# Carrying the state of a gated linear attention once per 128 tokens instead of once per 64

## The chip, the cores and the metric

The kernel runs on one core of a Trainium2 chip. TensorE multiplies matrices, VectorE (DVE), ScalarE (ACT) and GpSimd (POOL) do elementwise work, SyncE (SP) issues the loads. The metric is the device time of one execution in microseconds, median of several runs; less is better.

## The reference

A residual decoder layer for 512 tokens of width 1024: two token mixers side by side (GLA with 4 heads, keys of 128 and values of 256; HGRN2 with 8 heads, keys and values of 128), gates, an output projection, a convolutional feed-forward part, and norms. The change touches only the core of both mixers:

```python
def chunk_gated_linear_attn(q, k, v, log_g, scale):   # chunks of CHUNK = 64 tokens
    b = jnp.cumsum(log_g, axis=3)                     # within a chunk
    b_ref = b[..., CHUNK // 2 - 1:CHUNK // 2, :]
    b_last = b[..., -1:, :]
    scores = einsum(q * exp(b - b_ref), k * exp(b_ref - b))   # then causal mask
    o_intra = einsum(scores, v)
    chunk_state = einsum(k * exp(b_last - b), v)
    chunk_decay = exp(b_last)
    S_next = chunk_decay * S + chunk_state            # scan over the chunks
    o_inter = einsum(q * exp(b), S_prev)
    return o_intra + o_inter
```

After it come an RMS norm per head, a silu gate, the merge of both mixers and `merged @ w_out`.

## The kernel before

Everything large is a product in three terms: an fp32 matrix is split into a high part and a rest, `three` issues hi x hi, lo x hi and hi x lo. `unit` does one slice of 128 output columns over all 512 tokens: 24 matmuls of 512 columns. ScalarE makes `w_hi` from a loaded slice (`split_hi`), VectorE `w_lo` (`split_lo`); SyncE's next load into the ring of three raw buffers waits for `w_lo`. Before some loads SyncE also waits for a row of `ada_acc`, which VectorE adds up between its other work.

The mixers run as four groups (group 0 written out, groups 1 to 3 in a loop of the same code). A group has 18 units, n = 0 to 17, and three heads: h = 0 is a GLA head, h = 1 and 2 are HGRN heads. The order on every engine is written out by hand: each engine's `group` has a list of what it does ahead of or behind unit n. Between the units TensorE does small blocks: `turn` and `score` of head 0 behind unit 7, `chunk_states(0)` behind 8, `outputs` of head 0 behind 10, `turn` of heads 1 and 2 behind 11, `chunk_states` of head 1 behind 12 and of head 2 behind 13, `score` of both behind 14, `outputs` of both behind 15, and the sums of `ada_acc` behind 16. Behind unit 1 stand `low_rank` and the transposes of the group before (`merged_turn`). Units 2 to 5, 8 to 11 and 14 to 17 are quads that wait for all four `w_lo` of the quad.

A tile is 128 tokens, two chunks. The tensors of one head lie with the key channel on the partitions and the 512 tokens in the free dimension: `ks`, `qs` (scaled about the middle of the chunk, for the scores), `kp` (scaled to the end of the chunk, for the state), `qe` (scaled from its start, for the output from the state). ScalarE makes their exponentials (`exps`), VectorE multiplies `kp` and `ks` with the key (`times_k`), GpSimd `qs` and `qe` with the query (`times_q`). `turn` transposes `kp`, ScalarE takes it to `kT`. `score` makes four matmuls per tile, each with 32 array columns; VectorE copies the scores under the mask to `sT`. `chunk_states` multiplies `kT` with `v`, 64 rows (one chunk) at a time, seven times per head; VectorE runs the recurrence over seven states (`states`). `outputs` adds `sT` times `v` and, chunk by chunk, `qe` times the state, the latter with 64 array columns each. Matmuls on these operands are in plain fp32, and each shows as two records in the profile. `gla_rms` (ScalarE) squares and sums the GLA outputs, `gla_y` (VectorE) applies the norm and the gate; `outputs(1, 2)` overwrites the same PSUM banks and waits for `gla_y`.

## Time and profile before

| | |
|---|---|
| median of 3 runs | 943.22 us (942.72 to 943.66) |
| the profiled execution | 943.3 us, its span 941.6 us |
| granted TensorE clock, mean | 0.987 |
| TensorE busy | 911.9 us (97%) |
| VectorE, ScalarE, GpSimd busy | 501.3, 456.2, 155.6 us |
| chain that ended last | TensorE 87%, every other engine at most 3% |

Busy time of TensorE says that it had a matmul under way, not that it ran at its peak. The groups take the span from about 55 to 517 us; the output projection and the feed-forward part follow. The stretches of groups 1, 2 and 3 start at 171.23, 290.11 and 408.99 us, with the transposes of the group before behind unit 1. The third group below is group 2, from 290.11 to 408.99 us.

### The profile page before, as it was taken

What the parts mean: (1) busy time and instruction counts of PE and PEld (TensorE: products, weight loads), DVE (VectorE), ACT (ScalarE), POOL (GpSimd) and SP (SyncE); (2) the same over time, 40 slices, a digit from 0 to 9 for tenths busy, and PEclk for the clock granted to TensorE, in tenths of its full rate; (3) what the DMA queues carried; (4) which work ended last, traced back from release to release, by engine and by line L of the source; (5) the groups of instructions that cost most, each with busy time, mean ns of one, the idle gap of its engine ahead of it and who ended that gap; (6) DMA issues with size and microseconds to landing.
All of it is one profiled execution on the core that took longest, in us unless ns stands there. A gap on an engine that the chain in (4) does not pass through costs nothing.

```text
span 941.6 us, 13572 instructions
## 1 busy us (share of the span) xinstructions
PE 911.9 (97%) x4852; PEld 738.8 (78%) x4852; DVE 501.3 (53%) x690; ACT 456.2 (48%) x699; POOL 155.6 (17%) x146
## 2 busy tenths in 40 slices
PE   5998999999999999999999998999999999999997
PEld 4776788887888878888787776888888888888885
DVE  3545683457634476354764366744544544633327
ACT  5475554555645656456564263634333333523224
POOL 2010232002330123301232100121111121100000
PEclk8998999999999999999999999999999999999999
DMA  9946251662416624166230660433333333242202
GB/s 320 374 134 190 66 147 46 180 179 68 113 45 178 178 67 106 50 178 176 69 111 23 140 196 23 121 104 110 90 90 109 91 90 110 79 140 96 90 0 90
DMA packets 146830, 112.16 MB, mean 119 GB/s; under 512 B 4494, under 2 KB 138138, under 8 KB 146538
## 3 DMA queue, kind: packets, MB, share of 16 engines
q1 hardware_dynamic: 146288, 111.37, 39.9%
q8 instruction: 21, 0.34, 0.1%
q0 software_dynamic: 160, 0.20, 0.1%
q10 hardware_dynamic: 345, 0.13, 0.1%
q14 instruction: 16, 0.12, 0.1%
HBM read 107.49 MB, written 4.20 MB: 119 GB/s over the span
## 4 chain that ended last, share of the span: by engine, by line
PE 87%; DVE 3%; issue 3%; ACT 3%; DMA 2%; ACTq 0%; POOL 0%; SPq 0%; POOLq 0%; DVEq 0%
PE ps L1318 27%; PE ps L1320 26%; PE ps L1319 26%; PE ps L1438 2%; PE ps L1468 2%; DMA hres<-xT_saved_dram 1%; PE ps L1463 1%; PE ps L1352 1%; DMA raw<-in_w_in_dram 1%; DVE w_lo L893 1%; PE ps L1548 1%; PE ps L1420 1%; PE ps L1460 0%; ACT w_hi L557 0%; PE ps L1406 0%
## 5 line engine op out<-in xcount | busy, mean ns | idle before, releaser
L893 DVE TENSOR_TENSOR w_lo<-raw,w_hi 128x1024 fp32r<-128x1024 f32 x142 | 186.5, 1325 | 124.4 <-ACT w_hi L557 123.7
L1318 PE MATMUL ps<-h_hi,w_hi 128*128 128x512 f32 x608 | 238.9, 393 | 5.2 <-DVE h_lo L1235 3.3
L1320 PE MATMUL ps<-h_hi,w_lo 128*128 128x512 f32 x608 | 237.2, 390 | 0.0
L1319 PE MATMUL ps<-h_lo,w_hi 128*128 128x512 f32 x608 | 237.1, 390 | 0.0
L1318 PE MATMUL ps<-w_hi,h_hi 128*128 128x512 f32 x552 | 220.4, 399 | 5.4 <-DVE h_lo L933 3.8
L1319 PE MATMUL ps<-w_lo,h_hi 128*128 128x512 f32 x552 | 216.1, 392 | 0.0
L1320 PE MATMUL ps<-w_hi,h_lo 128*128 128x512 f32 x552 | 216.1, 391 | 0.0
L557 ACT ACTIVATE w_hi<-raw 128x1024 fp32r<-128x1024 f32 x142 | 146.9, 1052 | 70.7 <-PE ps L1320 48.8
L1318 PEld LDWEIGHTS ps<-h_hi,w_hi 128*128 128x128 f32 x608 | 114.5, 188 | 30.3 <-issue 4.5
L1319 PEld LDWEIGHTS ps<-h_lo,w_hi 128*128 128x128 f32 x608 | 114.6, 188 | 23.7 <-issue 0.2
L1320 PEld LDWEIGHTS ps<-h_hi,w_lo 128*128 128x128 f32 x608 | 114.4, 188 | 23.8
L1318 PEld LDWEIGHTS ps<-w_hi,h_hi 128*128 128x128 f32 x552 | 104.2, 189 | 32.9 <-issue 9.1
L1320 PEld LDWEIGHTS ps<-w_hi,h_lo 128*128 128x128 f32 x552 | 104.2, 189 | 22.5
L1319 PEld LDWEIGHTS ps<-w_lo,h_hi 128*128 128x128 f32 x552 | 104.4, 189 | 20.6
L824 ACT ACTIVATE conv<-ps,vecs 128x512 f32<-128x512 f32 x42 | 32.6, 778 | 130.4 <-PE ps L1320 130.4
L1247 DVE SCALAR_TENSOR_TENSOR conv<-ps,vecs,conv 128x511 f32<-128x511 f32 x44 | 32.9, 749 | 104.4 <-ACT conv L824 99.8
L544 POOL TENSOR_TENSOR prod<-conv 128x512 f32 x21 | 43.3, 2062 | 243.6 <-DVE conv L1251 243.6
L508 POOL TENSOR_TENSOR sg<-sg 128x256 f32<-128x256 f32 x32 | 26.1, 814 | 222.0 <-ACT sg L775 222.0
L775 ACT ACTIVATE sg<-ps 128x512 f32<-128x512 f32 x32 | 19.0, 595 | 76.4 <-PE ps L1320 76.3
L1061 DVE TENSOR_TENSOR gate<-ps,hnw_b 128x256 f32<-128x256 f32 x16 | 6.7, 421 | 55.2 <-ACT sg L775 55.2
L1251 DVE SCALAR_TENSOR_TENSOR conv<-ps,vecs,conv 128x510 f32<-128x510 f32 x44 | 32.9, 748 | 5.5 <-DVE conv L1247 0.2
L1092 DVE SCALAR_TENSOR_TENSOR ada_acc<-ada_w,cols,ada_acc 128x1024 f32<-128x1024 f32 x28 | 35.7, 1275 | 0.0
(205 smaller groups left out, 820.1 us busy)
## 6 DMA issues: line engine op xcount, KB each, us to landing
raw<-in_w_in_dram SPq DMA_DIRECT2D x68, 512.0 KB, 4.5
raw<-in_w_up_dram SPq DMA_DIRECT2D x44, 512.0 KB, 3.8
ada_w<-in_w_ada_dram SPq DMA_DIRECT2D x32, 512.0 KB, 4.4
raw<-in_w_down_dram SPq DMA_DIRECT2D x22, 512.0 KB, 3.3
ada_w<-in_w_ada_dram SPq DMA_DIRECT2D x8, 1024.0 KB, 9.1
raw<-in_w_out_dram SPq DMA_DIRECT2D x8, 512.0 KB, 4.7
x_tok<-in_x_dram SPq DMA_DIRECT2D x4, 512.0 KB, 5.2
w_first<-in_w_in_dram SPq DMA_DIRECT2D x8, 256.0 KB, 7.7
```

The lines of the kernel that those rows point to most:

```text
L508: pool.tensor_tensor(sg[:, j % 2, 0:2 * P], sg[:, j % 2, 0:2 * P], sg[:, j % 2, 2 * P:T], ALU.mult).then_inc(sides_made, 1)
L544: pool.tensor_tensor(prod[:, bass.ds(r * 3 + q, 1), :].rearrange("p a t -> p (a t)"), conv[:, 2 * q], conv[:, 2 * q + 1], ALU.mult).then_i ...
L557: act.activation(w_hi[:, slot(u)].rearrange("p k c -> p (k c)"), raw[:, raw_slot(u)].rearrange("p k c -> p (k c)"), ACT.Copy).then_inc(hi_ ...
L775: act.activation(sg[:, j % 2], bank, ACT.Sigmoid).then_inc(taken_act, 1)
L824: act.activation(conv[:, m], ps[:, m], ACT.Identity, bias=vecs[:, bass.ds(ch + V_CONVB, 1)], scale=vecs[:, bass.ds(ch + V_TAP2, 1)]).then_ ...
L893: dve.tensor_tensor(w_lo[:, slot(u)].rearrange("p k c -> p (k c)"), raw[:, raw_slot(u)].rearrange("p k c -> p (k c)"), w_hi[:, slot(u)].re ...
L1092: ins = dve.scalar_tensor_tensor(out=ada_acc[:], in0=ada_w[:, m % 2], scalar=c_act[:, m:m + 1], in1=ada_acc[:], op0=ALU.mult, op1=ALU.add)
L1247: dve.scalar_tensor_tensor(out=conv[:, m, 1:T], in0=ps[:, m, 0:T - 1], scalar=vecs[:, bass.ds(ch + V_TAP1, 1)], in1=conv[:, m, 1:T], op0=A ...
L1251: dve.scalar_tensor_tensor(out=conv[:, m, 2:T], in0=ps[:, m, 0:T - 2], scalar=vecs[:, bass.ds(ch + V_TAP0, 1)], in1=conv[:, m, 2:T], op0=A ...
L1318: pe.matmul(dst, a_hi, b_hi, start=start and i == 0, stop=False)
L1319: pe.matmul(dst, a_hi, b_lo, start=False, stop=False)
L1320: last = pe.matmul(dst, a_lo, b_hi, start=False, stop=stop and i == n - 1)
```

## The change

The state is carried once per tile. For that, within a tile:

- the keys of the first chunk are also decayed over the second (`kp` of the first chunk times the second chunk's decay), so that one matmul of 128 rows makes the tile's state; `decay2` is the product of both decays;
- the queries of the second chunk are decayed over the first, so that `qe` of the whole tile meets the state before the tile in one matmul;
- the second chunk sees the first by one more block of scores: `kx` (first chunk's keys, scaled to its end) with `qx` (second chunk's queries, scaled from its start), two more matmuls with 32 array columns per tile and head; the mask keeps this block now.

Heads 1 and 2 make their states in one block behind unit 13. `gla_rms` moves from ahead of unit 13's result to ahead of unit 14's, `gla_y` from n = 14 to behind the masks of n = 15.

```diff
@@ -164,7 +164,8 @@
         lb, omlb = cols[:, 18:26], cols[:, 26:34]
         a_ffn = cols[:, 34:42]
         ssq, rst = cols[:, 45:49], cols[:, 49:53]
-        qscale = cols[:, 53:54]
+        decay2 = cols[:, 42:54].rearrange("p (h t) -> p h t", t=TT)
+        qscale = cols[:, 58:59]
...
-        def gla_u(i):
-
-            a = ((i // 2) % 2) * 2 * P
-            return ps[:, B_STATE + i % 2 + 2 * (i // 4), a:a + 2 * P]
+        def u_of(w, t):
+
+            if w == 0:
+                return ps[:, B_STATE + t // 2, (t % 2) * 2 * P:(t % 2 + 1) * 2 * P]
+            return ps[:, B_STATE + w - 1, t * P:(t + 1) * P]
+
+        def by_chunk(ap, odd):
+
+            return ap.rearrange("p (t c i) -> p t c i", c=2, i=CHUNK)[:, :, odd]
+
+        def one_per_chunk(h, odd):
+
+            return decay[:, h].rearrange("p (t c) -> p t c", c=2)[:, :, odd:odd + 1].to_broadcast([P, TT, CHUNK])
...
             def times_q(g, h, q):
@@ -499,6 +510,10 @@
                 pool.wait_ge(exp_made, g * 15 + 5 * h + 4)
                 pool.tensor_tensor(qs[:, s], qs[:, s], q, ALU.mult).then_inc(qq_made, 1)
                 pool.wait_ge(exp_made, g * 15 + 5 * h + 5)
+                pool.tensor_tensor(qx[:, s], by_chunk(qe[:, s], 1), by_chunk(q, 1), ALU.mult).then_inc(qd_made, 1)
+                pool.tensor_tensor(by_chunk(qe[:, s], 1), by_chunk(qe[:, s], 1), one_per_chunk(h, 0), ALU.mult
+                                   ).then_inc(qd_made, 1)
+                pool.wait_ge(qd_made, g * 6 + 2 * h + 2)
                 pool.tensor_tensor(qe[:, s], qe[:, s], q, ALU.mult).then_inc(qq_made, 1)
...
                     if n == 12:
                         take_kT(g, 1)
                         take_kT(g, 2)
-                    if n == 13:
+                    if n == 14:
                         gla_rms(g)
                     if n == 16:
                         hgrn_rms(g)
...
             def times_k(g, h):
                 s = h % 2
-                for i, e in enumerate((kp, ks)):
-                    dve.wait_ge(exp_made, g * 15 + 5 * h + (1, 3)[i])
+                def with_key(dst, e, view):
                     if h == 0:
-                        ins = dve.tensor_tensor(e[:, s], e[:, s], key[:, 1], ALU.mult)
-                    else:
-                        ins = dve.scalar_tensor_tensor(out=e[:, s], in0=key[:, h - 1],
-                                                       scalar=omlb[:, bass.ds(g * 2 + (h - 1), 1)], in1=e[:, s],
-                                                       op0=ALU.mult, op1=ALU.mult)
-                    ins.then_inc(kk_made, 1)
+                        return dve.tensor_tensor(dst, e, view(key[:, 1]), ALU.mult)
+                    return dve.scalar_tensor_tensor(out=dst, in0=view(key[:, h - 1]),
+                                                    scalar=omlb[:, bass.ds(g * 2 + (h - 1), 1)], in1=e,
+                                                    op0=ALU.mult, op1=ALU.mult)
+                def first_half(ap):
+                    return by_chunk(ap, 0)
+                def whole(ap):
+                    return ap
+                dve.wait_ge(exp_made, g * 15 + 5 * h + 2)
+                d = decay[:, h].rearrange("p (t c) -> p t c", c=2)
+                with_key(kx[:, s], first_half(kp[:, s]), first_half).then_inc(kd_made, 1)
+                dve.tensor_tensor(decay2[:, h], d[:, :, 0], d[:, :, 1], ALU.mult).then_inc(kd_made, 1)
+                dve.tensor_tensor(first_half(kp[:, s]), first_half(kp[:, s]), one_per_chunk(h, 1), ALU.mult
+                                  ).then_inc(kd_made, 1)
+                dve.wait_ge(kd_made, g * 9 + 3 * h + 3)
+                with_key(kp[:, s], kp[:, s], whole).then_inc(kk_made, 1)
+                dve.wait_ge(exp_made, g * 15 + 5 * h + 3)
+                with_key(ks[:, s], ks[:, s], whole).then_inc(kk_made, 1)
...
                 dv = 2 * P if w == 0 else P
                 side = slice((w == 2) * P, (w == 2) * P + dv)
-                for i in range(NCH - 1):
-                    if i == 0:
+                for t in range(TT - 1):
+                    if t == 0:
                         dve.wait_ge(u_done, g * 3 + w + 1)
-                    u = gla_u(i) if w == 0 else ps[:, B_STATE + i % 2, (i // 2) * P:(i // 2 + 1) * P]
-                    if i == 0:
-                        ins = dve.tensor_copy(state[:, 0, side], u)
+                        ins = dve.tensor_copy(state[:, 0, side], u_of(w, 0))
                     else:
-                        dve.wait_ge(state_made, g * GROUP_STATES + 7 * w + i)
-                        ins = dve.scalar_tensor_tensor(out=state[:, i, side], in0=state[:, i - 1, side],
-                                                       scalar=decay[:, w, i:i + 1], in1=u,
+                        dve.wait_ge(state_made, g * GROUP_STATES + (TT - 1) * w + t)
+                        ins = dve.scalar_tensor_tensor(out=state[:, t, side], in0=state[:, t - 1, side],
+                                                       scalar=decay2[:, w, t:t + 1], in1=u_of(w, t),
                                                        op0=ALU.mult, op1=ALU.add)
                     ins.then_inc(state_made, 1)
...
                     if n == 9:
                         states(g, 0)
-                    if n == 13:
-                        states(g, 1)
                     if n == 15:
                         mask_scores(g, 1)
                         mask_scores(g, 2)
+                        for t in range(TT):
+                            gla_y(g, t)
                     for m in (HI_AT_FIRST if first else HI_AT).get(n, ()):
...
                         times_k(g, 2)
                     if n == 14:
+                        states(g, 1)
                         states(g, 2)
-                        for t in range(TT):
-                            gla_y(g, t)
                     rows_at = ADA_ROWS_FIRST if first else ADA_ROWS
...
                 pe.wait_ge(kk_made, g * 6 + 2 * h + 2)
                 pe.wait_ge(qq_made, g * 6 + 2 * h + 1)
+                pe.wait_ge(qd_made, g * 6 + 2 * h + 1)
                 half = CHUNK // 2
                 for t in range(TT):
                     for j in range(0, P, half):
                         i = slice(t * P + j, t * P + (j // CHUNK + 1) * CHUNK)
                         last = pe.matmul(ps[j:j + half, MISC_S[h], i], ks[:, h % 2, t * P + j:t * P + j + half],
                                          qs[:, h % 2, i], start=True, stop=True)
+                    for j in range(0, CHUNK, half):
+                        last = pe.matmul(ps[j:j + half, MISC_S[h], t * P + CHUNK:(t + 1) * P],
+                                         kx[:, h % 2, t, j:j + half], qx[:, h % 2, t], start=True, stop=True)
                 last.then_inc(scored, 1)
 
-            def chunk_states(g, w):
-
-                pe.wait_ge(kT_made, g * 3 + w + 1)
-                if w == 0:
+            def tile_states(g, ws):
+
+                pe.wait_ge(kT_made, g * 3 + ws[-1] + 1)
+                pe.wait_ge(state_made, g * GROUP_STATES + (TT - 1) * ws[0])
+                if ws[0] == 0:
                     pe.wait_ge(merged_made, g * 2)
-                    pe.wait_ge(y_made, g * 12)
-                pe.wait_ge(state_made, g * GROUP_STATES + 7 * w)
-                for i in range(NCH - 1):
-                    rows_ = slice(CHUNK * (i % 2), CHUNK * (i % 2) + CHUNK)
-                    if w == 0:
-                        u, dv = gla_u(i), slice(0, 2 * P)
-                    else:
-                        u, dv = ps[:, B_STATE + i % 2, (i // 2) * P:(i // 2 + 1) * P], slice((w + 1) * P, (w + 2) * P)
-
-                    last = pe.matmul(u, kT[rows_, w % 2, i // 2], v[rows_, i // 2, dv], start=True, stop=True)
-                last.then_inc(u_done, 1)
+                for w in ws:
+                    dv = slice(0, 2 * P) if w == 0 else slice((w + 1) * P, (w + 2) * P)
+                    for t in range(TT - 1):
+                        last = pe.matmul(u_of(w, t), kT[:, w % 2, t], v[:, t, dv], start=True, stop=True)
+                    last.then_inc(u_done, 1)
 
             def outputs(g, hs):
 
                 h = hs[-1]
                 pe.wait_ge(sT_made, g * 3 + h + 1)
                 pe.wait_ge(qq_made, g * 6 + 2 * h + 2)
-                pe.wait_ge(state_made, g * GROUP_STATES + 7 * (h + 1))
-                pe.wait_ge(y_made, g * 12 + (TT if hs[0] else 0))
-                rounds = [[(0, 0), (0, 2)], [(0, 1), (0, 3)]] if hs[0] == 0 else [[(h, t) for t in range(TT)] for h in (1, 2)]
-                for pairs in rounds:
-                    parts = []
-                    for h, t in pairs:
+                pe.wait_ge(state_made, g * GROUP_STATES + (TT - 1) * (h + 1))
+                pe.wait_ge(y_made, g * 12 + (TT if h else 0))
+                for h in hs:
+                    for t in range(TT):
                         if h == 0:
                             o = ps[:, B_O + t // 2, (t % 2) * 2 * P:(t % 2 + 1) * 2 * P]
                             dv, side = slice(0, 2 * P), slice(0, 2 * P)
                         else:
                             o = ps[:, O_B[t], (h - 1) * P:h * P]
                             dv, side = slice((h + 1) * P, (h + 2) * P), slice((h - 1) * P, h * P)
-                        if t == 0:
-                            for a in (0, CHUNK):
-                                pe.matmul(o[a:a + CHUNK], sT[:, h % 2, 0, a:a + CHUNK], v[:, 0, dv],
-                                          start=True, stop=a == 0)
-                        else:
-                            pe.matmul(o, sT[:, h % 2, t], v[:, t, dv], start=True, stop=False)
-                        parts.append((h, t, o, side))
-                    for h, t, o, side in parts:
-                        for i in (2 * t, 2 * t + 1):
-                            if i:
-                                last = pe.matmul(o[(i % 2) * CHUNK:(i % 2 + 1) * CHUNK],
-                                                 qe[:, h % 2, i * CHUNK:(i + 1) * CHUNK],
-                                                 state[:, i - 1, side], start=False, stop=True)
+                        last = pe.matmul(o, sT[:, h % 2, t], v[:, t, dv], start=True, stop=t == 0)
+                        if t:
+                            last = pe.matmul(o, qe[:, h % 2, t * P:(t + 1) * P], state[:, t - 1, side],
+                                             start=False, stop=True)
                 last.then_inc(o_done, len(hs))
...
                     if n == 8:
-                        chunk_states(g, 0)
+                        tile_states(g, (0,))
                     if n == 10:
                         outputs(g, (0,))
                     if n == 11:
@@ -1530,10 +1541,8 @@
                         turn(g, 1)
                         pe.wait_ge(sT_made, g * 3 + 1)
                         turn(g, 2)
-                    if n == 12:
-                        chunk_states(g, 1)
                     if n == 13:
-                        chunk_states(g, 2)
+                        tile_states(g, (1, 2))
                     if n == 14:
                         pe.wait_ge(kT_made, g * 3 + 3)
                         score(g, 1)
```

TensorE, behind unit 10 of group 0, the block `outputs(0)`. Before, products with `sT` and with the state come in two array widths:

```order
L1460 MATMUL ps<-v,sT 64x256 x2
L1463 MATMUL ps<-v,sT 128x256
L1468 MATMUL ps<-state,qe 64x256 x3
L1463 MATMUL ps<-v,sT 128x256 x2
L1468 MATMUL ps<-state,qe 64x256 x4
```

Now:

```order
L1478 MATMUL ps<-v,sT 128x256 x2
L1480 MATMUL ps<-state,qe 128x256
L1478 MATMUL ps<-v,sT 128x256
L1480 MATMUL ps<-state,qe 128x256
L1478 MATMUL ps<-v,sT 128x256
L1480 MATMUL ps<-state,qe 128x256
```

All are of the whole array, and seven take the place of twelve.

VectorE, n = 4 to 6 of a loop pass, around `times_k(0)`; `ada_acc` is the adaLN sum. Before:

```order
L893 TENSOR_TENSOR w_lo<-raw,w_hi 128x1024 x2
L1092 SCALAR_TENSOR_TENSOR ada_acc<-ada_w,cols,ada_acc 128x1024
L1012 TENSOR_TENSOR kp<-kp,key 128x512
L1012 TENSOR_TENSOR ks<-ks,key 128x512
L1092 SCALAR_TENSOR_TENSOR ada_acc<-ada_w,cols,ada_acc 128x1024
L893 TENSOR_TENSOR w_lo<-raw,w_hi 128x1024 x4
```

Now:

```order
L908 TENSOR_TENSOR w_lo<-raw,w_hi 128x1024 x2
L1116 SCALAR_TENSOR_TENSOR ada_acc<-ada_w,cols,ada_acc 128x1024
L1026 TENSOR_TENSOR kx<-kp,key 128x256
L1037 TENSOR_TENSOR cols<-decay 128x4
L1038 TENSOR_TENSOR kp<-kp,decay 128x4x64
L1026 TENSOR_TENSOR kp<-kp,key 128x512
L1026 TENSOR_TENSOR ks<-ks,key 128x512
L1116 SCALAR_TENSOR_TENSOR ada_acc<-ada_w,cols,ada_acc 128x1024
L908 TENSOR_TENSOR w_lo<-raw,w_hi 128x1024 x4
```

Three instructions stand ahead of the multiplication that makes `kp`; the next `w_lo` and `ada_acc` come behind them.

VectorE, n = 13 to 15 of a loop pass; `qry` is the silu of the queries, `state` the recurrence, `gate<-ps,rn,gate` is `gla_y`, `gate<-ps,hnw_b` the weighing of unit 14, `sT` the masks. Before:

```order
L1041 SCALAR_TENSOR_TENSOR state<-state,decay,ps 128x128 x6
L893 TENSOR_TENSOR w_lo<-raw,w_hi 128x1024
L1049 TENSOR_TENSOR qry<-ps,qry 128x512
L893 TENSOR_TENSOR w_lo<-raw,w_hi 128x1024
L1038 COPY state<-ps 128x128
L1041 SCALAR_TENSOR_TENSOR state<-state,decay,ps 128x128 x6
L1070 SCALAR_TENSOR_TENSOR gate<-ps,rn,gate 128x256 x4
L1061 TENSOR_TENSOR gate<-ps,hnw_b 128x256
L1024 MEMSET cols 128x1
L1025 COPY_PREDICATED sT<-causal,ps 128x512
L1024 MEMSET cols 128x1
L1025 COPY_PREDICATED sT<-causal,ps 128x512
```

Now:

```order
L1073 TENSOR_TENSOR qry<-ps,qry 128x512
L908 TENSOR_TENSOR w_lo<-raw,w_hi 128x1024
L1062 COPY state<-ps 128x128
L1065 SCALAR_TENSOR_TENSOR state<-state,cols,ps 128x128 x2
L1062 COPY state<-ps 128x128
L1065 SCALAR_TENSOR_TENSOR state<-state,cols,ps 128x128 x2
L1085 TENSOR_TENSOR gate<-ps,hnw_b 128x256
L1050 MEMSET cols 128x1
L1051 COPY_PREDICATED sT<-causal,ps 128x512
L1050 MEMSET cols 128x1
L1051 COPY_PREDICATED sT<-causal,ps 128x512
L1094 SCALAR_TENSOR_TENSOR gate<-ps,rn,gate 128x256 x4
```

The recurrences of both heads stand together and are shorter, and the four `gla_y` come behind the masks.

## Rows read from the trace of the kernel before

**Rows 1.** Table of stretches: us, busy us of each engine (count), granted clock, DMA.

```profile
290.11:408.99 118.88, 118.88 (x681) 95.39 (x681) 66.82 (x94) 67.26 (x108) 25.96 (x26) 1.00 0.40 115
...
85.00:90.00 5.00, 4.90 (x12) 3.83 (x13) 1.79 (x4) 3.59 (x5) 0.00 (x0) 0.50 1.05 297
```

**Rows 2.** Timeline of TensorE, small blocks of the third group: start, us, line, out<-in, shapes, count.

```profile
289.71 0.40 PE L1320 MATMUL ps<-h_hi,w_lo 128*128 128x512 f32 x1
289.95 1.02 PE L1489 MATMUL ps<-lrT,gk_g 128*128 128x512 f32 x2
290.81 1.04 PE L1480 MATMUL ps<-ident,gate 128*128 128x128 f32 x8
291.60 0.48 PE L1318 MATMUL ps<-w_hi,h_hi 128*128 128x512 f32 x1
```

**Rows 3.** The same timeline, state blocks of GLA and of HGRN head 1.

```profile
330.81 0.39 PE L1320 MATMUL ps<-w_hi,h_lo 128*128 128x512 f32 x1
331.13 1.99 PE L1438 MATMUL ps<-v,kT 64*128 64x256 f32 x14
333.05 0.50 PE L1318 MATMUL ps<-w_hi,h_hi 128*128 128x512 f32 x1
...
360.53 1.16 PE L1438 MATMUL ps<-v,kT 64*128 64x128 f32 x14
361.61 0.50 PE L1318 MATMUL ps<-h_hi,w_hi 128*128 128x512 f32 x1
361.95 0.39 PE L1319 MATMUL ps<-h_lo,w_hi 128*128 128x512 f32 x1
```

**Rows 4.** The same timeline, both output blocks and what follows.

```profile
344.19 0.65 PE L1460 MATMUL ps<-v,sT 128*64 128x256 f32 x4
344.77 0.70 PE L1463 MATMUL ps<-v,sT 128*128 128x256 f32 x2
345.40 1.08 PE L1468 MATMUL ps<-state,qe 128*64 128x256 f32 x6
346.41 1.13 PE L1463 MATMUL ps<-v,sT 128*128 128x256 f32 x4
347.47 1.08 PE L1468 MATMUL ps<-state,qe 128*64 128x256 f32 x8
348.49 0.50 PE L1318 MATMUL ps<-w_hi,h_hi 128*128 128x512 f32 x1
...
380.72 0.44 PE L1460 MATMUL ps<-v,sT 128*64 128x128 f32 x4
381.09 0.94 PE L1463 MATMUL ps<-v,sT 128*128 128x128 f32 x6
381.95 0.98 PE L1468 MATMUL ps<-state,qe 128*64 128x128 f32 x13
...
385.07 0.50 PE L1318 MATMUL ps<-w_hi,h_hi 128*128 128x512 f32 x1
```

**Rows 5.** The same timeline, scores of HGRN heads 1 and 2.

```profile
374.03 1.09 PE L1420 MATMUL ps<-qs,ks 128*32 128x64 f32 x64
375.06 0.50 PE L1318 MATMUL ps<-w_hi,h_hi 128*128 128x512 f32 x1
```

**Rows 6.** Waits of TensorE: us in total, times, longest.

```profile
PE ps L1406 <- DVE kp L1012: 2.2, 1, 2.2
PE ps L1318 <- DVE w_lo L893: 1.6, 1, 1.6
```

**Rows 7.** Timeline of GpSimd, then of VectorE, in group 0.

```profile
68.93 1.30 POOL L502 TENSOR_TENSOR qe<-qe,qry 128x512 f32<-128x512 f32 x1
...
69.02 3.43 DVE L893 TENSOR_TENSOR w_lo<-raw,w_hi 128x1024 fp32r<-128x1024 f32 x2 [2.18 <-ACT w_hi L557]
...
81.43 0.68 DVE L1012 TENSOR_TENSOR kp<-kp,key 128x512 f32<-128x512 f32 x1
```

**Rows 8.** Timeline of VectorE, last mask of the third group.

```profile
379.04 0.73 DVE L1025 COPY_PREDICATED sT<-causal,ps 128x512 f32<-128x512 uint32 x1
```

More of the change, by code:

```diff
@@ L74 @@
 O_B = (6, 7, 2, 3)
-GROUP_STATES = 3 * 7
+GROUP_STATES = 3 * (TT - 1)
 EARLY = 3 * P
@@ L211, in build @@
         decay = sm("decay", [P, 3, NCH])
+        kx = sm("kx", [P, 2, TT, CHUNK])
+        qx = sm("qx", [P, 2, TT, CHUNK])
         kT = sm("kT", [P, 2, TT, P])
         sT = sm("sT", [P, 2, TT, P])
-        state = sm("state", [P, NCH - 1, 2 * P])
+        state = sm("state", [P, TT - 1, 2 * P])
         gate = sm("gate", [P, 2 * TT, 2 * P])
@@ L300, in build @@
         exp_made = sem("exp_made")
+        kd_made = sem("kd_made")
+        qd_made = sem("qd_made")
         kk_made = sem("kk_made")
@@ L490, in _ @@
                                pattern=[[1, P]], channel_multiplier=-1).then_inc(mask_made, 1)
-            pool.wait_ge(mask_made, 4)
-            pool.memset(causal[0:CHUNK, CHUNK:P], 0.0).then_inc(mask_made, 1)
             pool.wait_ge(proj_done, 1)
@@ L1120, in group @@
                 if first:
-                    dve.wait_ge(mask_made, 6)
+                    dve.wait_ge(mask_made, 5)
                 for n in range(NU):
@@ L1545, in group @@
                         pe.wait_ge(ada_used, g * KT + KT)
-                        pe.wait_ge(state_made, g * GROUP_STATES + 21)
+                        pe.wait_ge(state_made, (g + 1) * GROUP_STATES)
                         for m in range(KT):
```

2 lines of the change are left out of this document (1 added, 1 removed).

## Prediction

> **What bounds the kernel now.** I read the table of stretches first. In the stretch of the third group TensorE is busy for all 118.88 us of 118.88, at a granted clock of 1.00 [rows 1]; the second group has the same length. Nothing but TensorE's own instruction stream sets the time of the four groups, so the change is worth what it takes out of that stream, minus any wait that it opens. The list of TensorE's waits shows the only two inside the groups: 2.2 us for `kp` and 1.6 us for `w_lo`, both in group 0 [rows 6]. After them the clock was granted at 0.50 for a stretch [rows 1], so a wait on TensorE costs more than its own length.
>
> Next the timeline of TensorE in that pass, to see what one small block costs. A block's time is from its first row to the next `L1318`. An fp32 matmul leaves two rows, so "x2" is one matmul. The row of `L1489` has 512 columns and takes 0.86 us to the next row [rows 2]: 1.67 ns per column. The eight rows behind it are four transposes of 128 columns and take 0.79 us up to the next unit [rows 2]: 0.20 us each. So a full 128x128 matmul runs at the column rate (0.21 us per 128 columns, 0.43 per 256) and its weight load is hidden.
>
> The blocks that the change rewrites are dearer than that. In `outputs(0)` one full matmul of 256 columns (`L1463` x2) takes 0.63 us, two (x4) take 1.06 [rows 4]: 0.43 each and a constant 0.20. Three of 128 columns (x6) take 381.95 - 381.09 = 0.86: 3 x 0.213 and 0.22 [rows 4]. The seven half-width state matmuls go two at a time: four rounds of 0.43 and about 0.2 in the state block (1.92) [rows 3]. So each change between whole-array and half-array matmuls costs 0.15 to 0.20 us, and a half-array block with seven matmuls needs four rounds of the time of a whole one. Before a half-array block there is also a gap: 330.81 + 0.23 = 331.04, but the block starts at 331.13; before the whole-array block of `L1489` there is none (289.71 + 0.23 = 289.94, start 289.95) [rows 2, 3].
>
> The Trainium skill ("TensorEngine Tiling (Array Packing)", Key Properties) says that a change of tiling mode, not of tile, drains TensorE. The constants of 0.20 us agree. If they belonged to the matmul instead, the sum would be that of the first rival below.
>
> **The change on TensorE, per group.** After it, the state blocks and the outputs are whole-array matmuls like those of the big units.
> - State block of GLA: 7 half matmuls, 1.92 us [rows 3]; now 3 whole ones of 256 columns, 3 x 0.427 = 1.28. Saves 0.64.
> - State blocks of HGRN heads 1 and 2: 2 x 1.08 = 2.16 [rows 3]; now one block of 6 x 0.213 = 1.28. Saves 0.88.
> - `outputs(0)`: 348.49 - 344.19 = 4.30 [rows 4]; now 7 x 0.427 = 2.99. Saves 1.31.
> - `outputs(1, 2)`: 385.07 - 380.72 = 4.35 [rows 4]; now 14 x 0.213 = 2.99. Saves 1.36.
> - The gap of 0.09 ahead of five blocks becomes 0.01: 0.40. One block is gone, and with it the slow restart behind it (0.34 us to the next matmul instead of 0.23 [rows 3]): 0.1.
>
> Together 4.7 us per group, 18.8 in four.
>
> Added on TensorE: per head and tile two more score matmuls, 64 columns each, into array columns 0 to 63. Two heads now take 1.03 us [rows 5]: eight tiles of one round of 64 columns (0.107) make 0.85, the rest is the constant. The added pair can't run beside the first pair, which has the same array columns, so each tile becomes two rounds: +0.427 per head. From below, if only the number of instructions counted, half of 0.5 = 0.26; from above, if everything doubled, 0.52. I take 0.43, since the round fits the row. Twelve heads, of which that of group 0's `score(0)` stands under a wait of TensorE: 11 x 0.427 = 4.7 us.
>
> **The change on VectorE and GpSimd.** DVE gets, per head, two multiplications over half a tile row (256 elements; half of `kp`'s 0.68 [rows 7], 0.4 with the start) and one of 4 elements (at most 0.2): 1.0 us; it loses 4 of 7 steps of the state recurrence in each head. POOL gets two of 256 elements per head, 0.65 to 0.75 each (half of `qe`'s 1.30 [rows 7] and up).
>
> In group 0 this isn't hidden. `turn(0)` waits for `kp` (2.2 us), and the next unit for the `w_lo` behind it on DVE (1.6 us) [rows 6]. The three new instructions stand right before `kp`, all of this DVE queue (`ks`, a row of `ada_acc`, `w_lo`, and TensorE behind it) moves by 1.0 us. There is a second path. At 69.02 DVE's two `w_lo` of 1024 elements take 3.43 us, where 512 elements of `kp` take 0.68 alone, so 0.7 us more than the size asks; the first began beside POOL's `qe` [rows 7], and I read that the one waits for the other's instruction to end. POOL now has two more instructions here, its last `qe` comes to lie beside DVE's first row of `ada_acc` (right behind 72.4), and SyncE issues the load of the next weights behind that row; those weights are what `kp`'s queue waits for. What that costs has no row: nothing if this single-input DVE instruction isn't stopped, 1.3 us (one `qe`) if it is. The nearest row is the stopped `w_lo`, so I take 1.3. So group 0 pays 2.3 us, between 1.0 and 3.3.
>
> The Trainium skill ("SBUF — State Buffer", Who interferes with whom) says the same of two-input instructions, and names `tensor_scalar` among those that can take the shared ports too. By it the 1.3 us holds; without it the sum is 1.3 us better.
>
> In the other groups the same work has cover. The mask of the last head ends at 379.04 + 0.73, 0.95 us before `outputs(1, 2)` starts at 380.72 [rows 4, 8]. Now TensorE comes there some 2 us earlier, and the four `gla_y` stand behind the masks instead of ahead of them; all that DVE does there is waited for by this block, since it overwrites the banks that `gla_y` reads. Against this, DVE has 12 state steps of 128 columns become 4, and ScalarE takes `qry` of the last `hq` unit before the norm sums instead of after them, which brings masks and `gla_y` forward with the TensorE work that they hang on. I get an end of `gla_y` 1 to 2 us before TensorE's wait. The queue of DVE behind `times_k(0)` (last weights of the quad after `score(0)`) is 0.9 us later, with about 1.5 us of margin. Both are thin; I count nothing for them in the sum.
>
> **The sum.** 18.8 - 4.7 - 2.3 = 11.8 us. The profiled execution took 943.3 us, 1.7 around its span of 941.6, and lies 0.1 above the median of the three runs, 943.22. All behind the groups hangs on TensorE's time, so it moves as a whole: 943.22 - 11.8 = 931.4.
>
> **The rivals.**
> 1. *The 0.20 us is part of each whole matmul's price.* Then a whole matmul costs 0.53 (1.06 / 2) and 0.287 (0.86 / 3) as the rows divide, the blocks are worth 2.4 us per group, and the result is 943.2 - 4 x 2.4 + 4.7 + 2.3 = 940.6. For it: these are the only whole matmuls of this kind. Against it: x2 with 0.63 and x4 with 1.06, and transposes at 0.20. Chance 0.10.
> 2. *One of the thin margins breaks.* TensorE waits 0.5 to 2 us in each of three groups for `gla_y` or for `w_lo`: 933 to 937, more if the clock falls after it. For it: margins of 1 to 2 us built from many terms, and DVE and POOL now meet more often. Against it: the longest of these chains starts at TensorE's own last blocks and moves with them. Chance 0.20.
> 3. *Slower than before.* The moved norm sums are the place: `gla_y` ends late in every group, TensorE stands before `outputs(1, 2)`, and the clock falls as at 85 us, where 12 matmuls then took 4.9 us [rows 1] instead of 12 x 0.23: 2.1 us more. From 11.8 / 4 = 3 us lost in each group it is no gain, which is `gla_y` 1 us late plus the clock; with 3 us it is 4 x 5.1 - 11.8 = 8.6 above, 951.8. Against it: the four `gla_y` are all that this chain gained, and more left it. Chance 0.04.
> 4. *More than forecast*: `ada_acc` isn't stopped and the new scores overlap with the next tile, 11.8 + 1.3 + 1.9 = 15, 928.2. Chance 0.10.
>
> The forecast itself keeps 0.56, with its own range of 929.5 to 933. The range 928.0 to 938.0 leaves out the first and third rivals and the ends of the others. Faster by over 0.2% (what a measurement here can tell): 0.94, all but the third rival and a remainder. Within 0.2%: 0.02. Slower: 0.04.
>
> **What would show it.** A group of 118.88 - 4.7 + 1.3 = 115.5 us with TensorE busy throughout. Blocks of 1.28, 1.28, 2.99 and 2.99 us; `outputs(0)` at 3.7 would be rival 1. Two heads of scores at 1.9 us. The two waits of group 0 together near 6 us instead of 3.8. A wait of TensorE at the first matmul of `outputs(1, 2)`, or at the unit behind `score(0)`, would be rival 2 or 3. A group over 118.88 us makes the prediction wrong as a whole.

## Result and the profile after

| | before | after |
|---|---|---|
| median | 943.44 us (942.72 to 945.30, 4 runs) | 927.38 us (926.26 to 929.29, 4 runs) |
| ratio | | 0.9829, 95% interval 0.9805 to 0.9853: -16.1 us |
| profiled execution, span | 943.3, 941.6 us | 929.29, 927.6 us |

The forecast was -11.8 us (931.4), its range 928.0 to 938.0; the result lies just below the range. One execution of a kernel in the experiments (the changed one with both edits of group 0) took 1841.88 us, twice the time of its five others, and stands in no ratio.

The time is best read in stretches from the first row of `low_rank` in one group to that row in the next, since the length of the start differs by up to 3 us from one execution to another whatever the kernel (that row lies between 55.8 and 58.7 us in the fourteen profiles). Worked out from the timelines:

| us | start to group 0 | group 0 | group 1 | group 2 | group 3, to its turn | rest |
|---|---|---|---|---|---|---|
| before | 57.2 | 113.9 | 118.9 | 118.9 | 115.3 | 417.5 |
| after | 58.5 | 108.8 | 115.1 | 115.1 | 111.7 | 418.4 |
| difference | +1.3 | -5.1 | -3.8 | -3.8 | -3.6 | +0.9 |

The four groups lose 16.2 us together (524.1 - 57.2 = 466.9 before, 509.2 - 58.5 = 450.7 after), as much as the ratio says. The first and last column are spread, not the change: three further profiles of kernels with the old blocks have a rest of 418.8 to 419.0, and the changed ones 417.3 to 418.7.

The stretch of the third group and then three stretches of one microsecond in group 0 of the changed kernel (columns as in [rows 1]):

```profile
282.60:397.71 115.11, 115.11 (x675) 96.27 (x675) 65.53 (x91) 67.28 (x108) 31.86 (x32) 1.00 0.41 118
...
84.00:85.00 1.00, 0.00 (x0) 0.01 (x1) 0.97 (x3) 1.00 (x3) 0.00 (x0) 1.00 0.00 0
85.00:86.00 1.00, 0.98 (x4) 0.71 (x4) 1.00 (x2) 0.92 (x2) 0.00 (x0) 0.51 0.00 0
...
88.00:89.00 1.00, 1.00 (x4) 0.84 (x5) 0.96 (x3) 1.00 (x2) 0.00 (x0) 0.78 0.82 238
```

The group answers to the first row of [rows 1]: 115.11 instead of 118.88 us, TensorE busy throughout at the full clock. GpSimd has six instructions more, VectorE three fewer.

The blocks of that group on TensorE's timeline, to be read beside [rows 3, 4]. An fp32 matmul leaves two rows.

```profile
323.96 1.46 PE L1460 MATMUL ps<-v,kT 128*128 128x256 f32 x6
325.07 0.58 PE L1341 MATMUL ps<-w_hi,h_hi 128*128 128x512 f32 x1
325.48 0.39 PE L1342 MATMUL ps<-w_lo,h_hi 128*128 128x512 f32 x1
...
336.17 1.03 PE L1478 MATMUL ps<-v,sT 128*128 128x256 f32 x4
337.03 0.59 PE L1480 MATMUL ps<-state,qe 128*128 128x256 f32 x2
337.46 0.59 PE L1478 MATMUL ps<-v,sT 128*128 128x256 f32 x2
...
339.00 0.58 PE L1341 MATMUL ps<-w_hi,h_hi 128*128 128x512 f32 x1
...
356.43 1.50 PE L1460 MATMUL ps<-v,kT 128*128 128x128 f32 x12
357.69 0.48 PE L1341 MATMUL ps<-w_hi,h_hi 128*128 128x512 f32 x1
...
363.32 0.30 PE L1444 MATMUL ps<-qs,ks 128*32 128x64 f32 x7
365.22 0.50 PE L1341 MATMUL ps<-w_hi,h_hi 128*128 128x512 f32 x1
...
370.80 0.61 PE L1478 MATMUL ps<-v,sT 128*128 128x128 f32 x4
...
373.84 0.48 PE L1341 MATMUL ps<-w_hi,h_hi 128*128 128x512 f32 x1
```

From the first row of each block to the next unit: 1.11, 2.83, 1.26 and 3.04 us, where 1.28, 2.99, 1.28 and 2.99 were forecast. Inside `outputs(0)` one whole matmul (two rows) follows the other at 0.43 us with no constant. The scores of two heads take 365.22 - 363.32 = 1.90 us [rows 5: 1.03], the forecast's 1.9.

TensorE's waits inside the groups, which answer to [rows 6]. Of the two one is left, and `w_lo` no longer stands there:

```profile
PE ps L1429 <- DVE kp L1026: 3.7, 1, 3.7
```

VectorE in group 0, to be read beside [rows 7] (start, us, line, instruction), then GpSimd there:

```profile
70.33 3.29 DVE L908 TENSOR_TENSOR w_lo<-raw,w_hi 128x1024 fp32r<-128x1024 f32 x2 [2.18 <-ACT w_hi L572]
73.54 1.78 DVE L1113 TENSOR_SCALAR ada_acc<-ada_w,cols 128x1024 f32<-128x1024 f32 x1
...
82.18 1.22 DVE L908 TENSOR_TENSOR w_lo<-raw,w_hi 128x1024 fp32r<-128x1024 f32 x1 [5.73 <-ACT w_hi L572]
83.32 0.42 DVE L1026 TENSOR_TENSOR kx<-kp,key 128x256 f32<-128x256 f32 x1
...
84.18 0.69 DVE L1026 TENSOR_TENSOR kp<-kp,key 128x512 f32<-128x512 f32 x1
...
86.59 1.22 DVE L908 TENSOR_TENSOR w_lo<-raw,w_hi 128x1024 fp32r<-128x1024 f32 x1
```

```profile
70.94 1.60 POOL L514 TENSOR_TENSOR qe<-qe,decay 128x256 f32<-128x256 f32 x1
72.61 2.15 POOL L517 TENSOR_TENSOR qe<-qe,qry 128x512 f32<-128x512 f32 x1
```

Row 0 of `ada_acc` takes 1.78 us beside GpSimd's `qe`, and three new instructions stand ahead of `kp`; both were forecast. Before `w_lo` at 82.18 VectorE sits idle for 5.73 us: it waits for raw load 10, the weights of unit 10, which SyncE issued at 75.72 us, right behind a load of `ada_w` that had to wait for row 0. "Row sum 0" below is this first row of `ada_acc`.

### The profile page after: what moved, and what is told of

It reads as the page before. It is cut to its first block, busy times and chain, and to the rows that moved or that the text cites. A ratio compares the mean times of both kernels' runs of the same rounds, so it can differ in the third digit from the quotient of the medians.

```text
span 927.6 us, 13516 instructions
## 1 busy us (share of the span) xinstructions
PE 897.6 (97%) x4828; PEld 743.4 (80%) x4828; DVE 497.0 (54%) x678; ACT 456.5 (49%) x699; POOL 182.2 (20%) x169
## 4 chain that ended last, share of the span: by engine, by line
PE 89%; DVE 3%; issue 3%; DMA 2%; ACT 2%; POOL 1%; ACTq 0%; SPq 0%; POOLq 0%; DVEq 0%
PE ps L1341 27%; PE ps L1343 27%; PE ps L1342 26%; DMA hres<-xT_saved_dram 2%; PE ps L1478 1%; PE ps L1375 1%; PE ps L1480 1%; PE ps L1460 1%; PE ps L1429 1%; PE ps L1444 1%; DMA raw<-in_w_in_dram 1%; PE ps L1557 1%; PE ps L1447 1%; PE ps L1362 0%; DVE h_lo L1194 0%
```

## Experiments

Of the 4.3 us that the forecast missed, theory A puts most in group 0: the stretch at half the clock there became shorter, and the wait for `w_lo` was covered. Rival B puts it in the sizes of the blocks (the constant per change of array form, the scores), rival C in chance, above all of the start-up.

Every kernel was timed beside the kernel before; "group 0" and "steady" (group 1 or 2) are the stretches of the table above, in its own profile. Medians of the changed kernel differ by up to 2 us from one set of executions to another, so the stretches carry the argument. Ratios are against the kernel before.

**The changed kernel again.** 

> The changed kernel unaltered, timed again beside the kernel before. Of the 14 to 16 us that the two profiles and medians put between the kernels, the forecast had 11.8. Theory A (the first group's clock and its covered wait made the rest) expects the same difference again, -15 to -16.5 us. Rival C (the difference is chance of the start-up, where the first profile of the changed kernel came to its first group 1.3 us later) expects it to come out elsewhere, below -12.5 or beyond -17.

Measured: 929.18 against 944.22 us, ratio 0.9828 (0.981 to 0.9845). By the medians this is -15.0 us, by the ratio -16.2 (-14.6 to -17.9). The stretches are sharper: group 0 took 108.84, steady 115.11, and the four groups together 450.8 us against 450.7 in the first profile. The gain inside the groups is there again to 0.1 us, so the start-up (rival C) falls as the cause of the miss.

**Filling the idle time of group 0.** Both kernels get matmuls that hold TensorE busy (`fill(19)` ahead of the turn; in the kernel before `fill(12)`, and `fill(8)` behind the scores):

```diff
                     if n == 7:
                         pe.wait_ge(z_made, g + 1)
+                        if first:
+                            pe.wait_ge(taken_act, 4)
+                            fill(19)
                         turn(g, 0)
                         score(g, 0)
...
+def fill(count):
+    for i in range(count):
+        pe.matmul(ps[:, B_STATE], h_hi[:, 0, 0:P], h_hi[:, 1], start=True, stop=True)
```

After: 

> The changed kernel with 19 idle-filling matmuls of 512 columns (4.05 us at the full clock) ahead of the first group's transposes of kp, where TensorE stood idle from 80.95 to 85.02 us; they write a bank that nobody reads and leave no work out. Theory A: the clock no longer falls in the first group, the score block there takes 1.0 instead of 1.87 us, and the w_lo wait of 1.6 us that the slow block covered comes back in part, so that the time moves by only -1.0 to +0.3 us. If the clock in that stretch plays no part, 0.

Before: 

> The kernel before with the same idle-filling matmuls in the first group, 12 ahead of the transposes of kp (TensorE idle 79.64 to 82.26 us) and 8 behind the score block (idle 83.4 to 85.1 us). Theory A: the stretch at half the clock (83.9 to 90.5 us) goes, unit 8 of the first group falls from 8.3 to 5.2-5.8 us, and the kernel gets 2.3 to 3.1 us shorter; the difference to the filled changed kernel is then 13 to 14 us, near the blocks and gaps alone. Rival B (all the error is in the blocks' sizes): less than 0.5 us of change here.

Measured: after, filled, 927.28 us, ratio 0.9834 (0.9808 to 0.986); before, filled, 942.19, ratio 0.998 (0.9968 to 0.9993). Group 0, after and then before (the kernel before without the filling is the third row):

```profile
56.41:164.95 108.54, 107.73 (x638) 89.99 (x637) 67.80 (x95) 64.53 (x105) 34.72 (x32) 1.00 0.47 136
```

```profile
58.40:170.08 111.68, 111.68 (x645) 89.31 (x644) 68.66 (x98) 64.32 (x105) 26.60 (x26) 1.00 0.45 131
```

```profile
57.21:171.07 113.86, 110.00 (x626) 87.36 (x625) 68.89 (x98) 64.31 (x105) 25.30 (x26) 0.97 0.44 128
...
84.00:85.00 1.00, 0.00 (x0) 0.00 (x0) 1.00 (x2) 0.98 (x3) 0.00 (x0) 0.50 0.27 33
...
90.00:91.00 1.00, 1.00 (x5) 0.82 (x4) 0.63 (x1) 0.98 (x2) 0.00 (x0) 0.68 1.12 370
```

With the clock held at 1.00 the kernel before loses 2.2 us of group 0, just under the 2.3 to 3.1 expected, since the filling overran there (unit 8 started 0.5 us later than without it); the changed kernel loses 0.3, where at the full clock a wait of 0.8 us for `w_lo` came back, as expected of it. The stretch at half the clock was thus worth 2.2 to 2.7 us before and 0.3 after. The gain of group 0 shrinks from 5.1 to 3.1 us, and rival B, by which nothing would have moved here, can hold only what is left.

**The added scores taken out.** The loop over `kx`, `qx` in `score` goes, four tiles with two matmuls each per head; so the second chunk of a tile no longer sees the first. 

> The changed kernel without the eight added score matmuls of each head (the second chunk of a tile doesn't see the first; everything else stays). By the forecast's price, 0.43 us per head for 11 heads, -4.7 us; for the first group's own block, at half the clock, up to 0.9 us more unless the w_lo wait comes back in its place: -4.7 to -5.6. If a half-array matmul cost only its columns (bound 0.26 us per head), -2.9 us.

Measured: 926.09 us, ratio 0.981 (0.9793 to 0.9827). A steady group took

```profile
165.95:279.78 113.83, 113.83 (x627) 94.95 (x626) 65.64 (x91) 67.32 (x108) 31.95 (x32) 1.00 0.42 119
```

115.11 - 113.83 = 1.28 = 3 x 0.427, the forecast's price to the digit. In group 0 the time rose instead, to 109.57: its waits were 3.9 for `kp` and again 0.8 for `w_lo`, since there the longer score block had stood in place of that wait. Unit 8 and the block behind it:

```profile
85.92 0.80 PE L1341 MATMUL ps<-w_hi,h_hi 128*128 128x512 f32 x1 [0.75 <-DVE w_lo L908]
...
93.22 1.46 PE L1457 MATMUL ps<-v,kT 128*128 128x256 f32 x6
```

Unit 8 starts 0.2 us later after the group's first row than with the added scores (29.5 against 29.4), but to the next block it takes 93.22 - 85.92 = 7.3 us instead of 5.8: the granted clock is at 0.50 from about 83 to 89.7 us, twice as long. That is 1.5 us for the clock against 0.9 saved in the scores of heads 1 and 2, and the rise of 0.8 is explained. With the added scores the low stretch was half as long, and TensorE had no second idle piece; that the one comes from the other is likely, not shown. The expectation's -4.7 missed this; it is -3.0 from the first row of group 0 to the end (866.3 against 869.3).

**The same matmuls with fewer changes of array form**, in the kernel before:

```diff
-rounds = [[(0, 0), (0, 2)], [(0, 1), (0, 3)]] if hs[0] == 0 else [[(h, t) for t in range(TT)] for h in (1, 2)]
+rounds = [[(0, 2), (0, 0)], [(0, 1), (0, 3)]] if hs[0] == 0 else [[(h, t) for t in (1, 2, 3, 0)] for h in (1, 2)]
```

> The kernel before with the same matmuls of outputs, of each set the first tile (whose scores come as two half-array matmuls) put last instead of first: outputs(0) goes 2, 0 and then 1, 3, outputs(1, 2) goes 1, 2, 3, 0. That takes away two changes between whole and half arrays in each of the two blocks and neither a matmul nor a column. The forecast's price (0.20 us per change) gives 4 x 0.20 = 0.8 us per group, a steady group of 118.0-118.1 instead of 118.9 us, and -3.2 us in all. Rival 1 of the forecast (the 0.20 us belongs to each whole-array matmul): 0.

Measured: 940.84 against 943.54 us, ratio 0.9972 (0.9961 to 0.9983). A steady group took

```profile
169.06:287.24 118.18, 118.18 (x681) 95.67 (x680) 66.49 (x94) 67.30 (x108) 26.07 (x26) 1.00 0.41 116
```

0.70 less for four changes, 0.175 us each (0.8 was expected). No matmul and no column was taken out, so the constant belongs to the change of form. Rival 1 of the forecast falls.

**The same price from the other side**, in the changed kernel:

```diff
-last = pe.matmul(o, qe[:, h % 2, t * P:(t + 1) * P], state[:, t - 1, side], start=False, stop=True)
+for a in (0, CHUNK):
+    last = pe.matmul(o[a:a + CHUNK], qe[:, h % 2, t * P + a:t * P + a + CHUNK],
+                     state[:, t - 1, side], start=False, stop=True)
```

> The changed kernel with each of the nine state matmuls of outputs (three per head) issued as two half-array matmuls, which share a slot of columns, so that the columns' time stays and only changes between whole and half arrays come in: 6 in outputs(0), 12 in outputs(1, 2). The forecast's 0.20 us per change gives +3.6 us per group (115.1 to 118.7) and +14.4 us in all. Rival 1 (0.20 us belongs to each whole-array matmul): 0. If each half takes its columns one after the other, 0.43 (head 0) and 0.21 us (heads 1, 2) come on top per pair, +2.6 us more per group.

Measured: 939.38 us, ratio 0.9954 (0.9936 to 0.9971). A steady group and the start of its `outputs(0)`:

```profile
288.49:406.71 118.22, 118.22 (x693) 95.75 (x692) 66.05 (x91) 67.26 (x108) 31.66 (x32) 1.00 0.40 115
```

```profile
342.22 1.02 PE L1478 MATMUL ps<-v,sT 128*128 128x256 f32 x4
343.17 0.65 PE L1481 MATMUL ps<-state,qe 128*64 128x256 f32 x4
343.76 0.70 PE L1478 MATMUL ps<-v,sT 128*128 128x256 f32 x2
```

3.11 more for 18 changes, 0.173 us each, and the two halves of a pair share one slot (343.76 - 343.17 = 0.59 = 0.43 and one change). Four fifths of the gain of a steady group (3.77) are undone by the form of nine matmuls.

**Loads and `kp` of group 0 earlier.** Two edits, the first on SyncE (L126), where the third load of `ada_w` (entry 2) goes behind raw loads 10 and 11, the second on VectorE:

```diff
-ADA_LOADS_FIRST = {8: (0,), 9: (1,), 10: (2,), 12: (3,), ...
+ADA_LOADS_FIRST = {8: (0,), 9: (1,), 12: (2, 3), ...
@@ vector, group
+                    if first and n == 6:
+                        dve.wait_ge(taken_act, g * N_ACT + act_count(5))
+                        times_k(g, 0)
                     for m in (HI_AT_FIRST if first else HI_AT).get(n, ()):
                         split_lo(U_MIX + m, g * NU + U_MIX + m + 1)
...
-                    if n == (6 if first else 5):
-                        dve.wait_ge(taken_act, g * N_ACT + act_count(5 if first else 1))
+                    if n == 5 and not first:
+                        dve.wait_ge(taken_act, g * N_ACT + act_count(1))
                         times_k(g, 0)
```

Both edits, before: 

> The kernel before with two edits in the first group alone: the third row block of w_ada is fetched behind the raw loads 10 and 11 instead of ahead of load 10, so that these aren't held on SP behind the first row sum, and VectorE makes kp and ks ahead of the splits of units 9 and 10. Theory A: kp is there before unit 7 ends, unit 8 starts 3 to 5 us earlier, the clock doesn't fall, and the first group takes 108 to 110 us instead of 113.9; the others are as they were: -4 to -6 us. If the waits of the first group are set elsewhere (the loads themselves), less than 2 us.

Both edits, after: 

> The changed kernel with both edits of the first group (loads and kp early). Theory A: no wait for kp, at most a short one for w_lo, no stretch at half the clock, first group 104.5 to 106 us (104 is a steady group less two units and a turn), -3 to -4.5 us. With the first group's waits gone from both kernels, the difference between this one and the kernel before with the same edits is the blocks alone: 3.8 us per steady group and 3.5 to 4.5 in the first, about 15 us. It would also be the best of all kernels here, near 924 us.

The loads alone, after: 

> The changed kernel with the loads' edit alone (third row block of w_ada fetched behind the raw loads 10 and 11). Raw load 10 was issued at 75.72 us, when row sum 0 (stopped by GpSimd to 1.78 us) was through; its own condition, the split of unit 7, is met about 3 us earlier. Expected: kp 2 to 3.5 us earlier, first group 105 to 107 us instead of 108.8, -2 to -4 us.

`kp` alone, after: 

> The changed kernel with VectorE's edit alone: in the first group kp and ks are made ahead of the splits of units 9 and 10, the loads stay. The 3.7 us wait for kp, the only one that TensorE's waits name in the first group, goes. Theory A (both waits come from the late raw loads 10 and 11): unit 8 starts only 0 to 1.2 us earlier, TensorE idles about as long as before, now ahead of unit 8 under a w_lo wait of 3 to 5 us, the clock falls behind it, and the first group takes 107.5 to 110 us instead of 108.8. Rival: the kp wait itself cost the time, first group 105 or less.

| kernel | median us | ratio (95%) | group 0 | TensorE's waits there |
|---|---|---|---|---|
| before, both | 938.81 | 0.9941 (0.9924 to 0.9958) | 107.15 | none |
| after, both | 920.87 | 0.976 (0.9747 to 0.9773) | 103.38 | none |
| after, loads | 921.52 | 0.9772 (0.9754 to 0.9789) | 103.38 | none |
| after, `kp` | 928.48 | 0.9836 (0.9817 to 0.9856) | 109.85 | w_lo 4.1 |

Group 0 of "before, both", then of "after, both":

```profile
58.29:165.44 107.15, 107.15 (x626) 85.56 (x624) 68.87 (x98) 64.30 (x105) 26.22 (x26) 1.00 0.46 136
```

```profile
55.83:159.21 103.38, 103.38 (x620) 86.43 (x618) 67.73 (x95) 64.53 (x105) 34.23 (x32) 1.00 0.49 143
```

And "after, `kp`": the wait that takes the place of the one removed, and the clock behind it:

```profile
PE ps L1344 <- DVE w_lo L908: 4.1, 1, 4.1
```

```profile
85.00:86.00 1.00, 0.00 (x0) 0.00 (x0) 0.33 (x1) 1.00 (x2) 0.00 (x0) 0.59 0.23 49
...
91.00:92.00 1.00, 1.00 (x4) 0.81 (x3) 0.56 (x1) 0.98 (x2) 0.00 (x0) 0.50 1.07 379
```

With every wait of group 0 gone from both kernels, the change is worth 107.15 - 103.38 = 3.77 us there, the same as in a steady group. In all three kernels with the new load order group 0 came out 0.9 to 1.6 us shorter than even the low end of what was expected. So group 0's waits, with the clock behind them, cost 113.9 - 107.15 = 6.7 us before and 108.8 - 103.38 = 5.4 after. Taking away the `kp` wait alone gains nothing, as expected: unit 8 still needs the weights of the late raw loads, TensorE stands idle later, and the clock falls for longer. Unit 8 starts 1.0 us earlier after the group's first row (28.3 against 29.4), but from its start to the next block it takes 7.9 us instead of 5.8, and the group comes out 1.0 longer. With the loads moved alone neither wait is left: the load order is the cause behind both. "After, loads" and "after, both" beat both given kernels, by 22.0 and 22.7 us against the kernel before.

**The norm sums where they were.** `gla_rms` at ScalarE's step 13 and `gla_y` at VectorE's step 14 again. 

> The changed kernel with the sums of squares of the first mixer and gla_y where they stood before the change (ScalarE's step 13 and VectorE's step 14). The forecast counted the move at nothing, since outputs(1, 2) finds gla_y 1 to 2 us ahead. Moved back they come earlier on both engines, ahead of mask_scores(1, 2) and the states, in front of which TensorE has little margin. Expected: within 0.3 us per group, within 1 us in all; if the move was needed, a wait for sT or state in every group and +1 us or more per group.

Measured: 928.41 us, ratio 0.9839 (0.9822 to 0.9857), no difference that medians can tell. The stretches can:

```profile
167.24:283.37 116.13, 115.28 (x676) 96.29 (x675) 65.49 (x91) 67.31 (x108) 31.58 (x32) 1.00 0.41 117
```

```profile
PE ps L1444 <- POOL qx L513: 1.5, 2, 0.9
```

Groups 1 and 2 take 1.0 and 0.8 us more; groups 0 and 3 nothing. The wait is not where either theory had it (for `sT` or `state`) but at the scores of the last heads, for the new `qx`. At most 0.3 us per group had been expected, and in two groups that missed. The profile shows the chain: ScalarE takes the last head's query (`qry`) behind the norm sums now, in the third group 78.0 us after the group's first row instead of 74.2, and GpSimd's `qx` and TensorE's scores follow. In the changed kernel, then in this one:

```profile
356.63 0.60 ACT L783 ACTIVATE qry<-ps 128x512 f32<-128x512 f32 x1 [2.09 <-PE ps L1343]
```

```profile
361.40 0.60 ACT L783 ACTIVATE qry<-ps 128x512 f32<-128x512 f32 x1
364.14 1.71 POOL L513 TENSOR_TENSOR qx<-qe,qry 128x256 f32<-128x256 f32 x1
```

`qx` of the last head ends at 365.85 us, and TensorE, idle for 0.66 us, goes on at 365.99.

**GpSimd's `qx` and `qe` of group 0, head 0, held until row sum 0 is through.**

```diff
                 pool.wait_ge(exp_made, g * 15 + 5 * h + 5)
+                if isinstance(g, int) and h == 0:
+                    pool.wait_ge(ada_used, 1)
                 pool.tensor_tensor(qx[:, s], by_chunk(qe[:, s], 1), by_chunk(q, 1), ALU.mult).then_inc(qd_made, 1)
```

> The changed kernel with GpSimd's qx and qe of the first group, head 0, held until row sum 0 of ada_acc is through on VectorE. The forecast put 1.3 us of the first group's cost on that row being stopped by GpSimd's qe; the profile has 1.78 us for it against 0.74 before. Expected by that: the row 0.7 to 0.8 us, raw load 10 and kp 1.0 us earlier, first group 107.4 to 108.2 us instead of 108.8, -0.6 to -1.4 us. If the row's length doesn't come from GpSimd, it stays at 1.8 us and nothing moves.

Measured: 923.75 us, ratio 0.9796 (0.9778 to 0.9815); group 0 106.56. VectorE there:

```profile
67.62 2.36 DVE L910 TENSOR_TENSOR w_lo<-raw,w_hi 128x1024 fp32r<-128x1024 f32 x2 [2.18 <-ACT w_hi L574]
69.90 0.75 DVE L1115 TENSOR_SCALAR ada_acc<-ada_w,cols 128x1024 f32<-128x1024 f32 x1
```

The row falls from 1.78 to 0.75 as expected, but the pair of `w_lo` ahead of it falls too, from 3.29 to 2.36. Raw load 10 is issued 2.0 us earlier after the group's start (15.2 against 17.2 us), the `kp` wait is 1.7 instead of 3.7, and with these shorter waits the clock isn't lowered at all. The gain of 2.2 us is above what was expected of it, because only the row had been counted.

## Why the prediction missed

**The bound** held. TensorE's stream set all four groups, and the only waits inside them are in group 0.

**The savings of 4.7 us per group** were 5.05: a steady group fell by 3.77, and the scores in it cost 1.28. Whole matmuls run at their columns' rate with no constant, as the sum had it. The four blocks, from first row to next unit, came out at 8.24 us instead of 8.54, all of it at the ends of the 256-column blocks; against this the next unit's first matmul takes 0.1 us more in all than the restart of 0.34 that was counted. Of the 0.35 us per group that the sum lacked, 0.1 isn't located. Over four groups this is 1.4 us of the miss. The price of a change of form, read as 0.15 to 0.20 us, is 0.173 to 0.175 by two experiments. The Trainium skill ("TensorEngine Tiling (Array Packing)", Key Properties), cited for the drain at a change of mode, agrees with both: the time goes with the changes and not with the matmuls.

**The scores** cost 0.427 us per head, as forecast.

**"So group 0 pays 2.3 us" is the step that failed.** TensorE's timeline in group 0, before and then after (the last number is the idle time ahead of the row; the row of `L1438`, `L1460` is the next small block, behind unit 8):

```profile
82.26 0.63 PE L1406 MATMUL ps<-ident,kp 128*128 128x128 f32 x4 [2.23 <-DVE kp L1012]
82.82 0.65 PE L1420 MATMUL ps<-qs,ks 128*32 128x64 f32 x32
85.10 0.79 PE L1318 MATMUL ps<-w_hi,h_hi 128*128 128x512 f32 x1 [1.63 <-DVE w_lo L893]
...
93.37 1.99 PE L1438 MATMUL ps<-v,kT 64*128 64x256 f32 x14
```

```profile
85.02 1.09 PE L1429 MATMUL ps<-ident,kp 128*128 128x128 f32 x4 [3.69 <-DVE kp L1026]
...
87.89 0.74 PE L1341 MATMUL ps<-w_hi,h_hi 128*128 128x512 f32 x1
88.46 0.39 PE L1342 MATMUL ps<-w_lo,h_hi 128*128 128x512 f32 x1
...
93.71 1.46 PE L1460 MATMUL ps<-v,kT 128*128 128x256 f32 x6
```

- `kp` comes 1.5 us later after the group's first row (82.26 - 57.21 = 25.05, then 85.02 - 58.52 = 26.50), not 2.3. The mechanism was right: raw load 10 is issued 0.9 us later behind the stopped row, and VectorE's additions ahead of `kp` take 0.9. But the row was stopped for 1.04 us, not 1.3, the pair of `w_lo` ahead of it, which was stopped before as well, shrank by 0.14, and the load landed 0.3 us faster (5.35 us against 5.66).
- Unit 8 also starts 1.5 us later (29.4 against 27.9). Of the 1.6 us `w_lo` wait nothing is left, because the longer score block, at half the clock, stands in its place; the unit couldn't have started before `w_lo`'s end in any case (86.59 + 1.22 = 87.81; it starts at 87.89).
- The clock was left out. Before, TensorE idled in two pieces and ran twelve matmuls of unit 8 at half the clock, 0.43 us each; from the start of unit 8 to the next block it took 93.37 - 85.10 = 8.3 us. After, the low stretch fell on the score block and ended in the first half microsecond of unit 8, and the same took 93.71 - 87.89 = 5.8. That is 2.4 us given back. The filled kernels show that it is the clock, and without the added scores the same piece of the changed kernel takes 7.3 us.

So where 2.3 us was entered, 1.5 - 2.4 = -0.9 belongs: a difference of 3.2. With the 1.4 us of the blocks this is the miss: 11.8 + 3.2 + 1.4 = 16.4, against the 16.2 of the four groups and the 16.1 of the ratio. (That group 0's score block stands under a wait, which keeps 0.4 us off the bill, was in the sum and held.)

The prediction saw the low clock in [rows 1] and said that a wait costs more than its own length. But it priced the clock only in the slower rival, and not for the wait that was already there and would move. That the low stretch came to lie on small work is luck of this schedule: with the waits gone from both kernels the change is worth 3.8 us in group 0, not 5.1.

**The moved norm sums and the margins**, counted at nothing, were worth nothing as a loss: no group but the first has a wait. In the third group the last `gla_y` ends at 368.9 us, 1.9 before `outputs(1, 2)` starts at 370.80, within the 1 to 2 us that the prediction gave. The move did do something, however: without it two groups wait 1.5 us together for `qx`, so a margin of the kind of rival 2 was close. The prediction had named ScalarE's `qry` ahead of the norm sums, but for the masks and `gla_y`, not for the scores. Rival 1's number was also wrong by itself: with 0.53 and 0.287 per whole matmul the items of the sum give 2.2 us per group, not 2.4, and 941.4, not 940.6; its price of 0.20 us per matmul fell in any case. Rival 4's number (928.2) is the nearest to the result, but both of its reasons are false: `ada_acc` is stopped and the scores don't overlap.

## What to carry to other kernels

Before a wait is priced, read the granted clock behind it and ask how the change moves both: a wait that gets longer can cost less if small work fills its end, and one that is removed alone may come back at the next instruction. Follow a wait to the DMA issue behind it (here a load queued behind another transfer's condition); moving one entry of a table there gave more than the kernel's wait list promised. Count changes between whole-array and half-array matmuls as instructions of their own (here 0.17 us each).

## Unexpected on the hardware

- The granted clock fell from 2.4 to 1.2 GHz (1.00 to 0.50 in the rows) after TensorE had been idle in group 0, though not after every such idle. With waits of 1.7 and 1.2 us (the kernel that holds GpSimd back) it stayed at 1.00; with 2.2 and 1.6 it was at 0.50 from about 84 to 90.5 us; with one of 3.7, from 85 to 88.3; with one of 4.1, from about 85 to 92; with 3.9 and 0.8 (without the added scores), from about 83 to 89.7. It came back soonest where TensorE was busy without a gap from the moment of the fall. What decides the length was not tried.
- Instructions of VectorE and GpSimd in group 0 lengthen one another: two `w_lo` take 3.29 to 3.43 us beside them and 2.36 without, a `tensor_scalar` of 1024 elements 1.78 and 0.75; GpSimd's own `qe` takes 2.15 there and 1.28 without. The Trainium skill ("SBUF — State Buffer", Who interferes with whom) names both kinds of instruction, and the trace agrees.
